# First layer's mixer woven into its input product: attention and retention by head pairs

## The chip, the cores and the metric

The kernel runs on one core of one Trainium2 chip. The metric is the device time of one execution in microseconds, lower is better; the median of several runs is compared. The kernel before took 1972.54 us (median of 3 runs, 1969.43 to 1974.33).

## What is computed

The reference is a stack of blocks on a sequence of 512 positions of width 1024, in float32: a first block (pooling, stick-breaking attention, memory attention), then two layers of mixer and convolutional GeGLU feed-forward. The change touches only the mixer of the first of these two layers, which is cut here to what matters:

```python
def retention_na_mixer(hn, w_in, ret_decay_logit, ret_gn_g, na_rpb, w_out):
    proj = hn @ w_in                                   # 512 x 1024 @ 1024 x 3584
    rq, rk, rv, rg, nq, nk, nv = jnp.split(proj, ...)  # seven parts of 512 columns, 8 heads x 64
    rq = rotary(rq); rk = rotary(rk) * 64 ** -0.5
    # decay gamma[0] for keys at or before the query, gamma[1] for keys after it
    y = bidir_scan(rq, rk, rv, rv, log_gamma[0], log_gamma[1])
    mu, var = mean and variance of y over the 64 channels of a head
    y = (y - mu) * rsqrt(var + EPS) * ret_gn_g
    ret_out = silu(rg) * y
    # 8 x 64 grid; each query sees all 8 rows and 16 columns around its own, with a bias by distance
    na_out = neighborhood_attention(nq, nk, nv, na_rpb)   # softmax
    return concatenate([ret_out, na_out]) @ w_out         # 512 x 1024 @ 1024 x 1024
```

After it, `x = x + rms_norm(m)`, and the feed-forward.

## The kernel before, in words

Activations lie with features on the 128 partitions and the 512 positions along the free dimension. A product is made by tiles of 128 output features. Each weight tile (128x1024, 512 KB) is a slot of a ring of five (RING): SyncE loads it (L264) as soon as slot q-5's product is done (slot_done), ScalarE makes its high part w_hi (hi_to, L271), VectorE the low part w_lo (lo_to, L278), and TensorE computes high x high, high x low and low x high for eight k (three, L305 to L311), 24 matmuls of 512 columns into one PSUM bank. split_ahead says how far ahead of tile t the splits are: it is an order written by hand into the programs of ScalarE and VectorE, and each engine's program is strictly in order. Normed products (in1, in2, up0, ...) start with a lead of several tiles that go k by k, while the input is still being split into a_hi and a_lo; other products start their first tile k by k.

The stage around the change, in order. "in2" has 28 tiles (four each of retention's Q, K, V, gate, and attention's Q, K, V), in banks (4 + t) % 8; VectorE evacuates each with a multiplication by the norm into p2 (L1955) and signals evac. tile_gone waits for such an evacuation. When all 28 are gone, retention runs: rotary by a swap matrix on TensorE, with cosine products on POOL and sine products on VectorE (ret_pe, ret_pool, ret_dve), V transposed (vt2), then head by head: scores of 128 keys by 512 queries in four banks, multiplied by the decay strip (weigh, L619), value matmuls (L516), evacuation (keep, L625). The strips come from the table dist by log_decay (L609, L610) and an exponential. Then the group norm over all four tiles (means by a ones matrix L526, squares, variances L529, Ln, Exp, and a refinement on VectorE, L409 to L415, L650). Then attention: V is cut into column windows and transposed (nvw, vna), and 16 units (head, half of the columns) go through scores (L692), bias, shift and maximum (L767, L771), exponential (L744), scaling by the inverse sum on VectorE (L775, L778), transposes of the weights (L702), a copy (L785), values (L715), and evacuation (L792). POOL adds bias and column mask (L756). Then the mixed tensor is split (split_mix2_act, split_mix2_dve) and "out2" starts, eight tiles one after another.

Matmuls of the mixer are in plain float32, which the trace records as two passes each. Q, K and V of a head take 64 partitions, two heads share a tile of 128.

Of the kernel before, what the change touches and what calls it, by code (L numbers as in the profile page):

```python
# [6 lines left out]
ACT = mybir.ActivationFunctionType  # L7
# [39 lines left out]
LEAD = {"in1": 2, "in2": 4, "up0": 4, "xbc": 4, "up1": 4}  # L47
# [4 lines left out]
def tile_home(name, t):  # L52
    if name == "xbc":
        return (4 + t + (1 if t >= 4 else 0) + (3 if t >= 14 else 0)) % 8
    if name == "z":
        return t % 2
    return (4 + t) % 8 if name in LEAD else t % 4

# [42 lines left out]
RET_Q, RET_K, RET_V, RET_G, NA_Q, NA_K, NA_V = 0, 4, 8, 12, 16, 20, 24  # L101
STRIP = 2 * S - P
# [26 lines left out]
def build(nc, dr, ctx, start):  # L129
# [27 lines left out]
    vt2 = at("vt2", [P, TT, RH * DH], ST + 56)  # L157
    aw2 = at("aw2", [P, 2, TT, S], ST + 64)
    strip = at("strip", [P, 2, STRIP], ST + 80)
    dist = at("dist", [P, STRIP], ST + 87)  # L160
    rope = at("rope", [P, 2, S], ST + 90.5)
    rtmp = at("rtmp", [P, 2, S], ST + 94.5)
    dec = at("dec", [P, 5, 16], ST + 98.5)
    gsq = at("gsq", [P, 4, S], 80)
    grs = at("grs", [P, 4, S], 88)
    ghalf = at("ghalf", [P, S], ST + 94.5)
    vna = at("vna", [P, 4, 2, NH * DH], ST + 64)
    bt = at("bt", [P, 2, ROWS, RPB_W], ST + 80)
    bm = at("bm", [P, 2, 4, ROWS, KEYW], ST + 84)
    cmask = at("cmask", [P, 4, KEYW], ST + 92)  # L170
    nprob = at("nprob", [P, 2, 2, ROWS * KEYW], ST + 92.5)
    npt = at("npt", [P, 2, 4, P], ST + 96.5)
    nstat = at("nstat", [P, 4, 32], ST + 100.5)
    nvw = at("nvw", [P, 4, 4, ROWS * KEYW], 64)
# [85 lines left out]
    def load_slot(sp_, q):  # L260
        name, t, part = SLOTS[q]
        if q >= RING:
            sp_.wait_ge(slot_done, q - RING + 1)
        sp_.dma_start(raw[:, q % RING, 0:slot_width(q)],  # L264
                      dr["w_" + name][t][:, part * 8 * P:part * 8 * P + slot_width(q)]).then_inc(w_load[q % RING], 16)
# [39 lines left out]
    def three(name, t, k, rhs_hi, rhs_lo, width, stop):  # L305
# [3 lines left out]
        nc.tensor.matmul(out, wh, rhs_hi[:, k, :], start=k == 0, stop=False)  # L309
# [174 lines left out]
    swap_done, cos_done, sin_done, rot_done = sem("swap_done"), sem("cos_done"), sem("sin_done"), sem("rot_done")  # L484
    strip_l, strip_e = sem("strip_l"), sem("strip_e")
    rz, ra, ry, ryc = sem("rz"), sem("ra"), sem("ry"), sem("ryc")

    g_mean, g_cent, g_sq, g_var, g_ln, g_done = sem("g_mean"), sem("g_cent"), sem("g_sq"), sem("g_var"), sem("g_ln"), sem("g_done")

    KEY_ORDER = (1, 2, 3, 0)  # L490

    def ret_pe(pe):
        for t in range(8):
            if t >= 4:
                pe.wait_ge(sin_done, t - 3)
            nc.tensor.matmul(bank[4 + t % 4][:, :], C["swap"], p2[:, t, :], start=True, stop=True).then_inc(swap_done, 1)
        for i in range(4):
            for j in range(TT):
                mm = nc.tensor.transpose(bank[i][:, j * P:(j + 1) * P], p2[:, RET_V + i, j * P:(j + 1) * P], C["ident"])
            mm.then_inc(vtp, 1)  # L500
        pe.wait_ge(vtc, 2 * TT)
        pe.wait_ge(rot_done, 8)

        def scores(h):
            b, th = DH * (h % 2), h // 2
            for j in KEY_ORDER:
                if j == 0 and h >= 2:
                    pe.wait_ge(ryc, h - 1)
                nc.tensor.matmul(zbank(h, j)[:, :], p2[b:b + DH, RET_K + th, j * P:(j + 1) * P], p2[b:b + DH, RET_Q + th, :],  # L509
                                 start=True, stop=True).then_inc(rz, 1)  # L510
# [1633 lines left out]
```

## Time and profile before

| | us |
|---|---|
| median of 3 runs | 1972.54 |
| the profiled execution, its own time | 1972.36 |
| its span | 1970.3 |
| TensorE busy | 1833.3 |
| VectorE busy | 1195.0 |
| ScalarE busy | 758.1 |
| POOL busy | 189.7 |

Times in a profile are microseconds from the span's start. PE is TensorE's matmuls, PEld its weight loads, DVE VectorE, ACT ScalarE, POOL GpSimd. L12 is line 12 of the kernel. In a row, "out<-in" are the names of what is written and read (p is p2), "x8" counts instructions, and in brackets stands how long the engine was idle before, and which instruction ended that. PEclk is the granted clock of TensorE, 1.00 being full speed.

### The profile page before, as it was taken

How to read it: one execution, taken by the hardware profiler on the slowest of the kernel's cores; microseconds unless marked ns; L12 is line 12 of the kernel's file. 1: busy time of each engine (PE TensorE's matmuls, PEld its weight loads, DVE VectorE, ACT ScalarE, POOL GpSimd, SP SyncE). 2: the span in 40 equal slices, each digit the busy share in tenths (PEclk: the TensorE clock that was granted, in tenths of full speed). 3: DMA queues.
4: the chain of work that ended last, by engine and by line, in shares of the span. 5: the costliest groups of instructions: out<-in, count | busy, mean ns of one | idle time of the engine just before them, and what ended most of it. 6: DMA issues, size and time to landing. Idle time of an engine off the chain costs nothing.

```text
span 1970.3 us, 20662 instructions
## 1 busy us (share of the span) xinstructions
PE 1833.3 (93%) x8186; PEld 1418.2 (72%) x8186; DVE 1195.0 (61%) x1647; ACT 758.1 (38%) x1278; POOL 189.7 (10%) x212
## 2 busy tenths in 40 slices
PE   7998989999878989999998999999989989999996
PEld 5885558887335768888886778677757868888885
DVE  4445554434868668866434699765676368866424
ACT  4235433212122335444323345446554245444321
POOL 0301200001123001111000000022022001111000
PEclk9999989999887989999999999999989999999998
DMA  5331002432001122333332222210001223233331
GB/s 199 97 96 54 1 11 75 137 97 85 0 13 30 64 70 93 98 96 100 98 96 83 81 75 96 65 33 24 33 32 54 96 76 96 96 97 97 95 99 62
DMA packets 42751, 147.86 MB, mean 75 GB/s; under 512 B 5152, under 2 KB 6304, under 8 KB 42528
## 3 DMA queue, kind: packets, MB, share of 16 engines
q1 hardware_dynamic: 39168, 138.43, 21.9%
q10 hardware_dynamic: 3488, 8.12, 1.2%
q8 instruction: 65, 1.06, 0.2%
q14 instruction: 30, 0.25, 0.0%
HBM read 144.44 MB, written 2.10 MB: 74 GB/s over the span
## 4 chain that ended last, share of the span: by engine, by line
PE 78%; DVE 14%; ACT 4%; issue 2%; DMA 1%; POOL 1%; ACTq 0%; DVEq 0%; POOLq 0%
PE bank L309 21%; PE bank L310 21%; PE bank L311 21%; DVE cv L1375 3%; DVE w_lo L278 2%; PE bank L509 2%; PE bank L516 1%; PE bank L1476 1%; PE bank L927 1%; PE bank L935 1%; ACT em L1576 1%; DVE bank L474 1%; PE bank L1437 1%; PE bank L920 1%; PE bank L1458 1%
## 5 line engine op out<-in xcount | busy, mean ns | idle before, releaser
L278 DVE TENSOR_TENSOR w_lo<-raw,w_hi 128x1024 fp32r<-128x1024 f32 (+1 forms) x264 | 336.6, 1277 | 532.7 <-ACT w_hi L271 532.6
L309 PE MATMUL bank<-a_hi,w_hi 128*128 128x512 f32 x1504 | 603.9, 402 | 36.1 <-DVE a_lo L374 27.8
L311 PE MATMUL bank<-a_hi,w_lo 128*128 128x512 f32 x1504 | 589.9, 392 | 0.0
L310 PE MATMUL bank<-a_lo,w_hi 128*128 128x512 f32 x1504 | 589.9, 392 | 0.0
L271 ACT ACTIVATE w_hi<-raw 128x1024 fp32r<-128x1024 f32 (+1 forms) x264 | 274.9, 1044 | 517.0 <-DMA raw<-in_w_in 172.6
L309 PEld LDWEIGHTS bank<-a_hi,w_hi 128*128 128x128 f32 x1504 | 285.7, 190 | 105.3 <-issue 22.4
L310 PEld LDWEIGHTS bank<-a_lo,w_hi 128*128 128x128 f32 x1504 | 285.6, 190 | 65.3 <-issue 6.7
L311 PEld LDWEIGHTS bank<-a_hi,w_lo 128*128 128x128 f32 x1504 | 285.0, 190 | 60.3
L309 PE MATMUL bank<-g_hi,w_hi 128*128 128x512 f32 x352 | 136.9, 389 | 0.0
L310 PE MATMUL bank<-g_lo,w_hi 128*128 128x512 f32 x352 | 136.9, 389 | 0.0
L311 PE MATMUL bank<-g_hi,w_lo 128*128 128x512 f32 x352 | 136.9, 389 | 0.0
L836 ACT ACTIVATE u<-bank,par 128x512 f32<-128x512 f32 x88 | 68.6, 780 | 176.2 <-DVE bank L474 176.2
L879 POOL TENSOR_TENSOR gv<-u 128x512 f32<-128x512 f32 x44 | 57.1, 1298 | 600.0 <-DVE u L855 600.0
L1576 ACT ACTIVATE em<-bank,lbias 128x128 f32<-128x128 f32 x256 | 70.9, 391 | 30.8 <-PE bank L1459 30.5
L1712 DVE TENSOR_TENSOR em<-em,gmat 128x512 f32<-128x512 f32 x64 | 48.7, 774 | 46.5 <-ACT em L1576 46.4
L309 PEld LDWEIGHTS bank<-g_hi,w_hi 128*128 128x128 f32 x352 | 66.1, 188 | 13.8
L311 PEld LDWEIGHTS bank<-g_hi,w_lo 128*128 128x128 f32 x352 | 66.1, 188 | 13.7
L310 PEld LDWEIGHTS bank<-g_lo,w_hi 128*128 128x128 f32 x352 | 66.1, 188 | 13.6
L1375 DVE SCALAR_TENSOR_TENSOR cv<-bank,par,cv 128x510 f32<-128x510 f32 (+1 forms) x96 | 71.7, 747 | 2.5
L855 DVE SCALAR_TENSOR_TENSOR u<-bank,par,u 128x511 f32<-128x511 f32 x88 | 66.0, 750 | 3.1
L852 DVE SCALAR_TENSOR_TENSOR u<-bank,par,u 128x511 f32<-128x511 f32 x88 | 65.1, 740 | 0.0
L474 DVE TENSOR_TENSOR bank<-bank,nrm_u 128x512 f32<-128x512 f32 x88 | 60.8, 691 | 0.9 <-PE bank L311 0.9
(347 smaller groups left out, 2197.0 us busy)
## 6 DMA issues: line engine op xcount, KB each, us to landing
raw<-in_w_up SPq DMA_DIRECT2D x88, 512.0 KB, 3.4
raw<-in_w_in SPq DMA_DIRECT2D x52, 512.0 KB, 3.5
raw<-in_w_out SPq DMA_DIRECT2D x32, 512.0 KB, 3.5
raw<-in_w_down SPq DMA_DIRECT2D x32, 512.0 KB, 3.5
raw<-in_w_xbc SPq DMA_DIRECT2D x24, 512.0 KB, 3.5
raw<-in_w_z SPq DMA_DIRECT2D x16, 512.0 KB, 3.5
raw<-in_w_down SPq DMA_DIRECT2D x16, 384.0 KB, 3.1
x<-in_xT ACTq DMA_DIRECT2D x4, 512.0 KB, 7.1
```

What stands on the lines that cost most here:

```text
L271: nc.scalar.activation(w_hi[:, q % RING, 0:w], raw[:, q % RING, 0:w], ACT.Copy).then_inc(hi_done, 1)
L278: nc.vector.tensor_tensor(w_lo[:, q % RING, 0:w], raw[:, q % RING, 0:w], w_hi[:, q % RING, 0:w].bitcast(F32), ALU.subtract).then_inc(lo_do ...
L309: nc.tensor.matmul(out, wh, rhs_hi[:, k, :], start=k == 0, stop=False)
L310: nc.tensor.matmul(out, wh, rhs_lo[:, k, :], start=False, stop=False)
L311: return nc.tensor.matmul(out, wl, rhs_hi[:, k, :], start=False, stop=stop)
L474: nc.vector.tensor_tensor(tile_bank(name, t)[:, :], tile_bank(name, t)[:, :], r, ALU.mult).then_inc(scaled, 1)
L836: nc.scalar.activation(u[:, t % 4, :], tile_bank(name, t)[:, :], ACT.Identity, scale=pcol(f"ffn_w{layer}", 3 * t + 1), bias=pcol(f"ffn_b{l ...
L852: nc.vector.scalar_tensor_tensor(out=ut[:, 1:S], in0=pt_[:, 0:S - 1], scalar=pcol(w, 3 * t), in1=ut[:, 1:S], op0=ALU.mult, op1=ALU.add).th ...
L855: nc.vector.scalar_tensor_tensor(out=ut[:, 0:S - 1], in0=pt_[:, 1:S], scalar=pcol(w, 3 * t + 2), in1=ut[:, 0:S - 1], op0=ALU.mult, op1=ALU ...
L879: nc.gpsimd.tensor_tensor(gv[:, i % 2, :], u[:, 2 * i % 4, :], u[:, 2 * i % 4 + 1, :], ALU.mult).then_inc(prod, 1)
L1375: nc.vector.scalar_tensor_tensor(out=dst, in0=tile_bank("xbc", tile)[:, a + by:b + by], scalar=pcol("conv_w", 5 * tile + tap), in1=dst, op ...
L1576: e = nc.scalar.activation(em[:, n % 4, c * P:(c + 1) * P], bank[4 + n % 2][:, c * P:(c + 1) * P], ACT.Exp, bias=lbias[:, c, d, h:h + 1])
```

## The change

The order of in2's tiles becomes IN2_ORDER: attention's Q, K, V by head pair (tiles 0 to 11), retention's K, Q, V by head pair (12 to 23), the gates (24 to 27). Tiles 8 and up use only banks 0 and 1; banks 2 to 7 belong to the mixer. Before the first step TensorE waits until tile 7 is evacuated. After it, eight attention steps go between tiles 8 to 15: the scores of the next step for two heads (each on its own 64 partitions, into its own bank), the tile, the values of the step before, the next step's windows of V and this step's transposes. Scaling by the inverse sum moves from VectorE to ScalarE, which also evacuates the windows. K and V of attention are stored by columns, so that a window is contiguous and its separate copies (nvw) go; Q is stored by blocks, which POOL's reordering did. Then eight retention steps (pair, half of the keys) go between tiles 16 to 27: four scores, four values of the step before with the output of the pair in one bank, one or two tiles, the swaps and the turned V of the next pair. Cosine and sine are applied at evacuation by VectorE (the tables are multiplied by the norm once), and the swap is taken of the sine product and added. V is multiplied by a centring matrix (identity minus 1/64 within a head) where it was transposed; so y comes out with its mean taken off, and the mean matmuls and their subtraction go. The group norm runs pair by pair, one and a half pairs behind. At the end SiLU of the gates, and "out2" starts with a lead of four tiles k by k in the order of MIX2_ORDER: attention's half first, retention's half after it; the last pair's variance lies behind the first k.

```diff
-LEAD = {"in1": 2, "in2": 4, "up0": 4, "xbc": 4, "up1": 4}
+LEAD = {"in1": 2, "in2": 4, "out2": 4, "up0": 4, "xbc": 4, "up1": 4}
...
-    if name == "z":
+    if name == "z" or name == "in2" and t >= 8:
         return t % 2
...
+IN2_ORDER = ([first + p for p in range(PAIRS) for first in (NA_Q, NA_K, NA_V)]
+             + [first + p for p in range(PAIRS) for first in (RET_K, RET_Q, RET_V)]
+             + [RET_G + p for p in range(PAIRS)])
+NA_STEPS = 2 * PAIRS
+RET_STEPS = 2 * PAIRS
+RET_TILES = [(17,), (18, 19), (20,), (21, 22), (23,), (24, 25), (26,), (27,)]
+MIX2_ORDER = (4, 5, 6, 7, 0, 1, 2, 3)
...
-        return PLAN[name]["slot0"] + max(min(t, 5) + 8, t + AHEAD) if name in LEAD else last_slot(name, t) + AHEAD
+        return PLAN[name]["slot0"] + max(min(t, 4 if name == "in2" else 5) + 8, t + AHEAD) if name in SUMS else last_slot(name, t) + AHEAD
...
+    def na_scores(pe, s):
+        p, i = s // 2, s % 2
+        tile_gone(pe, "in2", max(IN2_AT[NA_Q + p], IN2_AT[NA_K + p]))
+        if s:
+            pe.wait_ge(ns, 2 * s)
+        for r in range(2):
+            c = 2 * i + r
+            for e in range(2):
+                mm = nc.tensor.matmul(bank[4 + e][:, r * 256:(r + 1) * 256], p2[HALF[e], NA_Q + p, c * P:(c + 1) * P],
+                                      window(NA_K + p, c, parts=HALF[e]), start=True, stop=True)
...
+    def na_values(pe, s):
...
+                for e in range(2):
+                    mm = nc.tensor.matmul(bank[2][HALF[e], c * P:(c + 1) * P], vna[:, s % 2, 2 * r + f, HALF[e]],
+                                          npt[:, e, 2 * r + f, :], start=f == 0, stop=f == 1)
...
+    def ret_turn_v(pe, p):
...
+        for j in range(TT):
+            mm = nc.tensor.matmul(bank[6 if p else 3][:, j * P:(j + 1) * P], p2[:, RET_V + p, j * P:(j + 1) * P], centre[:, :],
+                                  start=True, stop=True)
...
+    def ret_scores(pe, r):
...
+            for e in range(2):
+                nc.tensor.matmul(bank[4 + 2 * jj + e][:, :], p2[HALF[e], RET_K + p, j * P:(j + 1) * P], p2[HALF[e], RET_Q + p, :],
+                                 start=True, stop=True).then_inc(rz, 1)
...
+    def two_pe(pe):
...
+            tile_pe(pe, "in2", t, a_hi, a_lo)
+        tile_gone(pe, "in2", 7)
+        na_windows(pe, 0)
+        na_scores(pe, 0)
+        for s in range(NA_STEPS):
+            if s + 1 < NA_STEPS:
+                na_scores(pe, s + 1)
+            tile_pe(pe, "in2", 8 + s, a_hi, a_lo)
+            if s:
+                na_values(pe, s - 1)
+            if s + 1 < NA_STEPS:
+                na_windows(pe, s + 1)
+            na_turn(pe, s)
+            if s == NA_STEPS - 2:
+                ret_swaps(pe, 0)
+        ret_turn_v(pe, 0)
+        tile_pe(pe, "in2", 16, a_hi, a_lo)
+        na_values(pe, NA_STEPS - 1)
+        for r in range(RET_STEPS):
+            p, half = r // 2, r % 2
+            ret_scores(pe, r)
+            if r:
+                ret_values(pe, r - 1)
+            for n, t in enumerate(RET_TILES[r]):
+                tile_pe(pe, "in2", t, a_hi, a_lo)
+                if n == 0 and half and p + 1 < PAIRS:
+                    ret_swaps(pe, p + 1)
+                    ret_turn_v(pe, p + 1)
+            if half == 0 and p:
+                ret_variance(pe, p - 1)
+        ret_values(pe, RET_STEPS - 1)
...
+    def out2_pe(pe):
+        for n, k in enumerate(MIX2_ORDER):
+            pe.wait_ge(mixlo, KT + n + 1)
+            if n == 1:
+                ret_variance(pe, PAIRS - 1)
+            for t in range(LEAD["out2"]):
...
+                mm = three("out2", t, k, a_hi, a_lo, S, n == KT - 1, MIX2_ORDER[0])
...
+        for t in range(LEAD["out2"], KT):
+            if t >= 6:
+                pe.wait_ge(g_norm, PAIRS - 2 + t - 5)
+            tile_pe(pe, "out2", t, a_hi, a_lo)
...
+        act.wait_ge(nyc, MEM_HEADS + PAIRS)
+        act.wait_ge(slot_done, last_slot("in2", 27) + 1)
+        high(0)
+        high(1)
+        square(PAIRS - 1)
+        high(2)
+        high(3)
+        nc.scalar.preload_act_table(ACT.Silu)
+        for t in range(4):
+            tile_gone(act, "in2", IN2_AT[RET_G + t])
+            nc.scalar.activation(p2[:, RET_G + t, :], p2[:, RET_G + t, :], ACT.Silu).then_inc(silu_done, 1)
+        nc.scalar.preload_act_table_set(LOGEXP)
+        roots(PAIRS - 1)
...
+        for s in range(NA_STEPS):
+            if s:
+                turned(s - 1)
+            if s + 1 < NA_STEPS:
+                for e in range(2):
+                    shift(s + 1, e)
+                invert(s + 1, 0)
+            lo_to(dve, split_ahead("in2", 8 + s))
+            if s + 1 < NA_STEPS:
+                invert(s + 1, 1)
+            take(8 + s)
+            if s and s % 2 == 0:
+                keep_na(s // 2 - 1)
+            if s == 1:
+                decay_dve(dve)
+                dve.wait_ge(dist_load, 16)
+            if s in (3, 5):
+                log_decay(s // 4)
+        turned(NA_STEPS - 1)
+        rotate(0)
+        tile(16)
+        keep_na(PAIRS - 1)
+        for r in range(RET_STEPS):
+            p, half = r // 2, r % 2
+            weigh(r)
+            if half == 0 and p:
+                keep_ret(p - 1)
+            for n, t in enumerate(RET_TILES[r]):
+                tile(t)
+                if n == 0 and half and p + 1 < PAIRS:
+                    rotate(p + 1)
+            if half == 0 and p + 1 < PAIRS:
+                log_decay(2 * p + 2)
+                log_decay(2 * p + 3)
+            if half and p:
+                norm(p - 1)
+        low(0)
+        keep_ret(PAIRS - 1)
+        for n in range(1, 4):
+            low(n)
+        norm(PAIRS - 1)
```

## Rows read from the trace of the kernel before

**Rows 1.** The page, part 1: each engine's busy time, share of the span, instructions.

```profile
PE 1833.3 (93%) x8186; PEld 1418.2 (72%) x8186; DVE 1195.0 (61%) x1647; ACT 758.1 (38%) x1278; POOL 189.7 (10%) x212
```

**Rows 2.** Busy time by stretch: length, PE, PEld, DVE, ACT, POOL, clock, DMA.

```profile
375.00:484.00 109.00, 108.84 (x481) 89.81 (x479) 39.08 (x45) 22.29 (x21) 0.00 (x0) 1.00 0.30 97
484.00:654.00 170.00, 133.43 (x465) 69.84 (x465) 132.96 (x230) 45.35 (x110) 42.52 (x48) 0.86 0.06 16
590.00:654.00 64.00, 50.59 (x245) 36.04 (x245) 53.98 (x106) 20.44 (x70) 19.57 (x28) 0.79 0.09 25
...
1300.00:1400.00 100.00, 97.01 (x526) 69.53 (x522) 64.05 (x94) 51.34 (x123) 16.91 (x11) 0.98 0.13 41
```

**Rows 3.** Waits between 484 and 654 us: waiter, releaser, total, times, longest.

```profile
PE bank L702 <- DVE nprob L778: 14.0, 11, 6.4
```

**Rows 4.** Busy time by stretch, retention's first scores.

```profile
503.00:511.20 8.20, 7.90 (x14) 3.71 (x15) 6.20 (x9) 2.15 (x3) 0.00 (x0) 0.51 0.00 1
```

**Rows 5.** Timeline of TensorE and ScalarE: start, length, instruction, idle before it.

```profile
374.88 0.39 PE L309 MATMUL bank<-a_hi,w_hi 128*128 128x512 f32 x1
...
378.69 1.06 ACT L271 ACTIVATE w_hi<-raw 128x1024 fp32r<-128x1024 f32 x1 [4.63 <-DMA raw<-in_w_in]
...
653.96 0.47 PE L309 MATMUL bank<-a_hi,w_hi 128*128 128x512 f32 x1 [1.60 <-DVE a_lo L818]
```

**Rows 6.** Timeline of VectorE, evacuations of in2's tiles (4; 5 to 9; 10; 27).

```profile
380.93 0.69 DVE L1955 TENSOR_TENSOR p<-bank,nrm 128x512 f32<-128x512 f32 x1
...
386.30 3.08 DVE L1955 TENSOR_TENSOR p<-bank,nrm 128x512 f32<-128x512 f32 x5
...
391.61 0.68 DVE L1955 TENSOR_TENSOR p<-bank,nrm 128x512 f32<-128x512 f32 x1
...
484.07 0.68 DVE L1955 TENSOR_TENSOR p<-bank,nrm 128x512 f32<-128x512 f32 x1
```

**Rows 7.** Timeline of TensorE at full clock: means, variances; one attention unit.

```profile
561.96 3.70 PE L526 MATMUL bank<-p,cst 128*128 128x512 f32 x8 [0.79 <-DVE p L625]
565.50 3.60 PE L529 MATMUL bank<-gsq,cst 128*128 128x512 f32 x8
...
631.00 0.66 PE L702 MATMUL bank<-cst,nprob 128*128 128x128 f32 x4 [0.24 <-DVE nprob L778]
631.60 1.09 PE L715 MATMUL bank<-npt,vna 128*64 128x128 f32 x8
632.62 1.13 PE L692 MATMUL bank<-p 64*128 64x256 f32 x4
```

**Rows 8.** Timeline of TensorE: first scores of two heads; SSD's paired heads among products.

```profile
507.72 1.22 PE L509 MATMUL bank<-p 64*128 64x512 f32 x2
...
1302.71 0.40 PE L311 MATMUL bank<-a_hi,w_lo 128*128 128x512 f32 x1
1303.03 1.09 PE L1476 MATMUL bank<-em,xtok 128*64 128x128 f32 x16
1304.06 1.09 PE L1424 MATMUL bank<-cst,xbc 128*128 128x128 f32 x8
...
1306.30 0.47 PE L309 MATMUL bank<-a_hi,w_hi 128*128 128x512 f32 x1
1306.62 0.39 PE L310 MATMUL bank<-a_lo,w_hi 128*128 128x512 f32 x1
```

**Rows 9.** Groups by line: count, busy us, mean ns, idle before; POOL's biases of a head.

```profile
L767 DVE SCALAR_TENSOR_TENSOR nprob<-bank,bm 128x512 f32<-128x512 f32 x16 | 11.0, 690 | 11.8 <-PE bank L702 6.2 <-POOL bm L756 5.5
...
599.63 2.86 POOL L756 TENSOR_TENSOR bm<-bt,cmask 128x256 f32<-128x256 f32 x4 [4.33 <-DVE nprob L767]
```

**Rows 10.** Timeline: group norm of one tile on VectorE; ScalarE's four SiLU.

```profile
484.21 2.19 ACT L1872 ACTIVATE p<-p 128x512 f32<-128x512 f32 x4
...
569.53 0.68 DVE L409 TENSOR_SCALAR ghalf<-bank 128x512 f32<-128x512 f32 x1
...
572.43 0.75 DVE L650 SCALAR_TENSOR_TENSOR p<-p,par,grs 128x512 f32<-128x512 f32 x1
```

More of the change, by code:

```diff
@@ new lines, in na_windows, with na_turn @@
+    def na_windows(pe, s):
+        p, i = s // 2, s % 2
+        tile_gone(pe, "in2", IN2_AT[NA_V + p])
+        if s:
+            pe.wait_ge(nvc, s)
+        for r in range(2):
+            for f in range(2):
+                mm = nc.tensor.transpose(bank[3][:, (2 * r + f) * P:(2 * r + f + 1) * P],
+                                         window(NA_V + p, 2 * i + r, f * KEYW // 2, (f + 1) * KEYW // 2), C["ident"])
+        mm.then_inc(nvp, 1)
+    def na_turn(pe, s):
+        for e in range(2):
+            un = 2 * s + e
@@ new lines, in ret_values @@
+    def ret_values(pe, r):
+        p, half = r // 2, r % 2
+        pe.wait_ge(ra, 4 * (r + 1))
+        if r == 0:
+            pe.wait_ge(nyc, MEM_HEADS + PAIRS)
+        elif half == 0 and p >= 2:
+            pe.wait_ge(g_norm, p - 1)
+        for jj in range(2):
+            j = 2 * half + jj
+            for e in range(2):
+                mm = nc.tensor.matmul(bank[2 + p % 2][HALF[e], :], vt2[p % 2][:, j, HALF[e]], aw2[:, r % 2, 2 * jj + e, :],
+                                      start=j == 0, stop=j == TT - 1)
+        mm.then_inc(rv, 1)
@@ L794, in na_dve, with turned @@
-        shift(0)
-        for un in range(NU):
-            if un + 1 < NU:
-                shift(un + 1)
-            norm(un)
-            if un:
-                turned(un - 1)
-        turned(NU - 1)
-        keep(NH - 1)
+            nc.vector.reciprocal(nstat[:, 2, 2 * un:2 * un + 2], nstat[:, 1, 2 * un:2 * un + 2]).then_inc(nrec, 1)
+        def turned(s):
+            for e in range(2):
+                dve.wait_ge(ntp, MEM_UNITS + 2 * s + e + 1)
+                nc.vector.tensor_copy(npt[:, e, :, :].rearrange("p a q -> p (a q)"), bank[6 + e][:, :]).then_inc(ntc, 1)
@@ new lines, in low @@
+        def low(n):
+            k = MIX2_ORDER[n]
+            dve.wait_ge(mixhi, KT + n + 1)
+            nc.vector.tensor_tensor(a_lo[:, k, :], mix2(k), a_hi[:, k, :].bitcast(F32), ALU.subtract).then_inc(mixlo, 1)
+        for t in range(4):
+            tile(t)
+        nc.vector.scalar_tensor_tensor(out=centre[:, :], in0=C["ones64"], scalar=-1.0 / DH, in1=C["ident"], op0=ALU.mult, op1=ALU.add)
+        for t in range(4, 8):
+            tile(t)
+        for e in range(2):
+            shift(0, e)
```

592 lines of the change are left out of this document (292 added, 300 removed).

## The prediction

> **What bounds the kernel now.** The page comes first. TensorE is busy for 93% of the span, VectorE for 61%, ScalarE for 38% [rows 1]; so time is to be had only where TensorE waits or runs slowly. The table by stage says where. From 375 to 484 us (the product "in2" from its tile 8 on) TensorE is busy for 108.8 of 109 us at a granted clock of 1.00; from 484 to 654 us (retention, then neighbourhood attention, no product beside them) it is busy for 133 of 170 us at 0.86, while the other engines are busy for 133 (VectorE), 45 and 43 us; from 654 us ("out2") it is full again [rows 2]. So the mixer's 170 us are the place: 37 us of waits, and a lower clock on a part of what is left. The waits view names the longest: 14.0 us for VectorE's softmax scaling, L778 [rows 3]; others are for the group norm and for V's evacuation. Two levels of the clock occur: after the wait for V's evacuation the stretch from 503.0 to 511.2 us runs at 0.51, which is 1.2 GHz [rows 4]; 1.00 is 2.4 GHz [rows 2].
>
> I compare two lengths, both from the first matmul of in2's tile 8 (374.88 us) to the first of out2 (653.96 us [rows 5]). Before: 653.96 - 374.88 = **279.1 us**.
>
> **The change part by part, at the full clock.**
>
> *Product.* Tiles 8 to 27 stay. VectorE's takes at 391.61 and 484.07 us are 17 tiles apart, so one is 5.44 us [rows 6]; 20 x 5.44 = **108.8**. One matmul of it is 5.44 / 24 = 0.227 us.
>
> *Neighbourhood attention.* Eight steps of two heads replace 16 units. In a unit of before, two score matmuls start 1.37 us ahead of the turn with a wait of 0.24 in it, four transposes take 0.60 (631.00 to 631.60), four value matmuls 1.02 (631.60 to 632.62) [rows 7]. A step issues four scores, four value windows to transpose, eight transposes and eight value matmuls. Transposes: 12 x 0.15 = 1.80 a step. The eight value matmuls alternate between the heads' column halves. That form stands in the trace of before, in the later SSD stage: L1476, 16 passes (each f32 matmul is recorded as two) of 128x128, two column halves in turn, runs from 1303.03 to 1304.06, 1.03 us, where the unit's 8 passes take 1.02 [rows 7, 8]. So pairs run side by side: 1.03 a step instead of 2.04. Scores: 8 passes of 256 columns, two row halves in turn, into two banks. For row halves I have only the place where head 0's last scores meet head 1's first: two passes recorded from the same 507.72 us [rows 8]. I take them as paired: four slots of 0.214 us (half of a 512-column pass, below) and 0.17 for the rest, as L1476 has over its eight slots of 0.107: 1.03. Unpaired it would be 2.0. Sum: 8 x (1.80 + 1.03 + 1.03) = **30.9**.
>
> *Retention.* A 512-column f32 matmul is two passes: 8 passes run from 561.96 to 565.50 us, 0.885 a matmul [rows 7]. Per head pair: two swaps 1.77; V turned and centred by four 128-column matmuls, priced as L715's eight passes, 1.02; 8 scores and 8 values in pairs, each group of four 4 x 0.43 + 0.17 = 1.88, so 4 x 1.88 = 7.5 (4 x 0.885 = 3.54 a group if unpaired). Four variances, one of them later: 3 x 0.885. The four mean matmuls and their centring are gone. Sum: 4 x (1.77 + 1.02 + 7.5) + 2.7 = **43.9**.
>
> *Changes of shape.* L1476 starts 0.32 us after the product matmul before it instead of 0.23, and 0.32 again leads back from transposes [rows 8]: 0.09 each. Those around the packed groups are in the 0.17; 20 returns to a product tile cost 20 x 0.09 = **1.8**. The Trainium skill (TensorEngine Tiling (Array Packing), section Key Properties) says that changing the tiling mode drains TensorE, which speaks against weaving: there are some 56 changes now. By these rows a change is about 0.1 us, 5.6 us in all, and that is what the sum holds; without a drain the time would be 5.6 us lower.
>
> *The start.* TensorE now needs tile 7 evacuated before the first window is turned (bank 3), and VectorE's program for tile 4 still splits weight slot 12 ahead of the take. That slot's buffer is free only when tile 7 is done. In the trace: ScalarE's split at 378.69 after the transfer, VectorE's behind it, the take of tile 4 at 380.93 [rows 5, 6]. The takes of tiles 5 to 7 follow at 0.60 (five in 3.08 us [rows 6]); tile 7 is gone at 383.4: **8.5 us** idle. Then scores(1) waits for both shifts of step 0: multiply-add, reduce, multiply-add are 0.72 + 0.60 + 0.69 [rows 9], **2.1 us** with the signal. After such a wait the clock is at 1.2 GHz for some 7.8 us of work [rows 4], which costs half of it: **3.9**. NA_Q, NA_K and NA_V are now stored permuted; nothing in the trace writes with an 8-element stride, so a take is 0.68 to twice that, and I keep 0.68 because the reordering copy L792 (16-element runs) took 0.68; the upper end costs 2.7 us at the start only. The bias loads move to the front: three more DMA issues at about 0.4 us on ScalarE's queue, ahead of splits with over 4 us of idle [rows 5]: nothing.
>
> *What the others must keep up with.* A step gives TensorE 5.44 + 3.86 + 0.1 = 9.4 us. VectorE in it: two shifts and reduces 2.7, two copies of turned weights 1.3, a weight split 1.2 (2.15 at most beside POOL), a take 0.7 (1.3 with the two rope products), strips and outputs 1.0: 7 to 8.5. ScalarE: four exponentials 2.0, four scalings 1.6, window 0.6, split 1.1: 5.3. POOL: the four biases 2.9 [rows 9]; up to twice that with its 8-element stride, still under 9.4. In order: turn(s-1) ends, copies 1.3, shifts 2.7, inverses and split end 6.4 us later, and the tile whose take is queued behind them ends 6.6 us later, so nothing waits; the slack is thin. In retention VectorE has 21 us per pair for TensorE's 16.3 + 10.3 + 0.9. The late points are weigh(1), (3) and (5), queued behind two strips (3.6 us); they end 2 to 3 us before the swaps that wait for them. Weight loads stay ahead: a tile's slot is freed one tile earlier, and the extra work only adds time. I take **0** for stalls inside, with 24 us (3 a step) as the upper bound.
>
> *The end.* a_hi can be overwritten only when tile 27 is done (T). VectorE then takes tile 27 and does norm(2) before low(0): 0.85, then 2.90 from the halving to the last multiply and 0.75 for that [rows 10], then 0.69, so out2 starts at T + 5.3. values(7), 1.9, lies in it: **3.4** net. The splits of before (idle 1.60 ahead of out2 [rows 5]) are covered. The lead's four k of the attention half take 4 x 12 x 0.227 = 10.9, plus the last variance 0.9: T + 17.1. The fifth k needs VectorE's keep, ScalarE's square, splits, a table load of 1.3, four SiLU of 2.2 in all [rows 10], a table load and roots (T + 13.9), VectorE's refine, gain, gate and split (T + 18.2): 1.2 of waiting. So out2 is **2.1** longer: the variance 0.9 and 1.2. The gates of pairs 0 to 2 on POOL (1.3 each) end by T + 10.5, and the silu itself no longer costs a stage.
>
> **Sum.** 108.8 + 30.9 + 43.9 + 1.8 + 8.5 + 2.1 + 3.9 + 3.4 = 203.3 us against 279.1: 75.8 less; with out2's 2.1, 73.7 less. The profiled execution took 1972.36 us (span 1970.3 and 2.1 around it), 0.2 under the median of the three runs. 1972.4 - 73.7 = 1898.7: I say **1899 us**. Where the gain comes from: 37 us of waits become 14 (8.5 + 2.1 + 3.4), the low clock costs 3.9 instead of some 16 (0.86 of 170 us withholds 24, a part of it in the waits), and pairing, with the means gone, saves some 42 us of TensorE's work.
>
> **Rivals.** (a) *Only the columns pair.* If 64-row scores run one after another, 8 x 0.97 + 8 x 1.66 = 21.0 us come back: 1920. If values don't pair either, another 8 x 1.01 + 8 x 1.66 = 21.4: 1941. For it: only one meeting of heads shows row halves together. Against: that meeting, and L1476, which does nothing else. (b) *VectorE becomes the bound in the attention steps.* Splits stretched to 2.15, slower strided writes, and the order on one queue: a step of 10.5 to 12.4 instead of 9.4 gives 1908 to 1923. For it: 0.2 us of slack in the walk. Against: operations on PSUM and the reduces are steady at 0.69 (L767 [rows 9]). (c) *Slower than before, by the clock.* The woven stretch is a mixture of f32 passes, transposes and tiles; if TensorE stayed at 1.2 GHz in it, its 185 us of work would double, 2084 us. The point of decision: 73.7 us of extra time, that is 147 us of the stretch run at the low level. For it: 590 to 654 us has 0.79. Against: there TensorE waits in each unit; 1300 to 1400 us, the same mixture with tiles, has 0.98 [rows 2]. (d) *The change hides more than I allow*: no clock loss at the start (3.9), the end waits covered (4.6), no cost of changes (5.6): down to 1885.
>
> **How the numbers follow.** Forecast, 1890 to 1908: 0.60. (b) 0.16. (a) 0.07 for rows alone, 0.03 for both. (d) below 1890: 0.06. Between 1923 and the old time by a mixture of these: 0.04. (c), or another loop of waits that eats it all: 0.04. The range for 8 in 10 takes the forecast, (b), rows of (a) and a part of (d): 1886 to 1923. About 0.3% (6 us) is what can be told from no change; every case but (c) is faster by more than that: faster 0.95, same 0.01, slower 0.04.
>
> **What the profile after would show.** Right: an idle of 8 to 9 us on TensorE after tile 7, ended by VectorE's take; then takes of product tiles 9 to 10 us apart in the attention steps; eight-pass groups of retention in about 1.9 us; a clock near 1.00 from 400 us on; out2 starting near 578 us. Wrong: groups of 3.6 us (a), TensorE waiting for VectorE's shifts or rope in most steps (b), granted clocks under 0.9 in the woven stretch (c), more than 6 us between tile 27 and out2.

## The result and the profile after

The changed kernel took **1894.97 us** (median of 4 runs, 1892.94 to 1897.02), the kernel before beside it 1972.59 us; the ratio is 0.961 (95% interval 0.960 to 0.963). The forecast was 1899, with 1886 to 1923 as its range. The profiled execution took 1892.94 us (span 1891.2).

The page of the kernel after, its part 1; TensorE is busy for 58 us less than in [rows 1]:

```profile
PE 1775.2 (94%) x8194; PEld 1387.4 (73%) x8194; DVE 1166.6 (62%) x1591; ACT 769.8 (41%) x1310; POOL 178.7 (9%) x199
```

The whole mixer now lies between 368.55 us (tile 7 done) and 571.53 (first matmul of out2). Busy time by stretch (length, PE, PEld, DVE, ACT, POOL, clock, DMA), to be read against [rows 2]:

```profile
375.00:394.00 19.00, 13.89 (x58) 10.27 (x58) 11.73 (x20) 7.37 (x23) 6.05 (x8) 0.63 0.11 30
394.00:470.00 76.00, 76.00 (x479) 59.07 (x479) 57.16 (x97) 38.95 (x96) 18.12 (x20) 1.00 0.24 76
470.00:572.00 102.00, 98.92 (x420) 62.37 (x419) 67.17 (x93) 24.56 (x30) 0.00 (x0) 1.00 0.17 57
```

Where before had 133 of 170 us busy at a clock of 0.86, TensorE is now full at 1.00 from 394 us to tile 27's end; what is left of waiting lies at the two ends. All its waits from 325 to 626 us (waiter, releaser, total, times, longest):

```profile
PE bank L594 <- DVE p L853: 9.2, 1, 9.2
PE bank L322 <- DVE a_lo L932: 3.9, 2, 3.1
PE bank L582 <- DVE nprob L867: 2.2, 1, 2.2
```

**The measure used from here on** is the length of the stage in each profile: from the first matmul of in2 to the first of up0, the next product after out2. Before it is 706.68 - 330.45 = 376.2 us, after it is 626.36 - 324.12 = 302.2, so 74.0 us less. It is steadier than a whole run: in2 starts at 324.1 to 332.7 us in the profiles of all these kernels, in which nothing ahead of in2 differs. The medians of the kernel before, timed beside them in four series, are 1972.59, 1968.34, 1970.78 and 1971.49.

### The profile page after: what moved, and what is told of

The parts are those of the page before. It is cut to its first block, busy times and chain, and to the rows that moved or that the text cites. A ratio compares the mean times of both kernels' runs of the same rounds, so it can differ in the third digit from the quotient of the medians.

```text
span 1891.2 us, 20686 instructions
## 1 busy us (share of the span) xinstructions
PE 1775.2 (94%) x8194; PEld 1387.4 (73%) x8194; DVE 1166.6 (62%) x1591; ACT 769.8 (41%) x1310; POOL 178.7 (9%) x199
## 3 DMA queue, kind: packets, MB, share of 16 engines
q8 instruction: 65, 1.06, 0.2%
## 4 chain that ended last, share of the span: by engine, by line
PE 80%; DVE 12%; ACT 5%; issue 1%; DMA 1%; ACTq 0%; POOL 0%; DVEq 0%
PE bank L322 22%; PE bank L323 22%; PE bank L324 22%; DVE cv L1552 4%; DVE w_lo L291 2%; PE bank L1653 1%; PE bank L1104 1%; PE bank L1112 1%; ACT em L1753 1%; PE bank L657 1%; DVE bank L487 1%; PE bank L1614 1%; PE bank L1097 1%; PE bank L670 1%; PE bank L1635 1%
## 5 line engine op out<-in xcount | busy, mean ns | idle before, releaser
L291 DVE TENSOR_TENSOR w_lo<-raw,w_hi 128x1024 fp32r<-128x1024 f32 (+1 forms) x264 | 337.5, 1281 | 460.6 <-ACT w_hi L284 460.3
```

The source lines that it names most:

```text
L291: nc.vector.tensor_tensor(w_lo[:, q % RING, 0:w], raw[:, q % RING, 0:w], w_hi[:, q % RING, 0:w].bitcast(F32), ALU.subtract).then_inc(lo_do ...
```

## The experiments

Each kernel is the changed one with one edit ("after, again" has none, and both_ends has two). Stage lengths and times; the number of timed runs is 4, or 2 for those marked *:

| kernel | stage, us | against after | median, us | ratio to before |
|---|---|---|---|---|
| after, again | 302.3 | | 1896.33 | 0.962 (0.960 to 0.965) |
| rows_in_blocks* | 302.3 | 0.0 | 1895.98 | 0.962 (0.958 to 0.966) |
| cols_in_blocks* | 306.4 | +4.2 | 1896.13 | 0.962 (0.959 to 0.965) |
| head_by_turns* | 330.3 | +28.0 | 1921.83 | 0.975 (0.972 to 0.978) |
| scale_on_vector | 301.6 | -0.7 | 1895.14 | 0.961 (0.960 to 0.963) |
| early_take | 298.0 | -4.3 | 1889.28 | 0.959 (0.957 to 0.961) |
| earliest_take | 292.2 | -10.1 | 1886.20 | 0.957 (0.955 to 0.958) |
| kept_busy | 300.3 | -2.0 | 1893.84 | 0.961 (0.959 to 0.964) |
| early_norm_end | 302.7 | +0.4 | 1898.46 | 0.964 (0.961 to 0.966) |
| own_square_buffer | 299.7 | -2.6 | 1890.95 | 0.959 (0.958 to 0.961) |
| out2_lead_one* | 313.1 | +10.9 | 1906.00 | 0.967 (0.964 to 0.970) |
| both_ends | 289.3 | -13.0 | 1880.30 | 0.954 (0.952 to 0.955) |

In "after, again" in2 starts at 326.36 us, and from the end of tile 7 to out2 it is 203.1 us again: the start wanders by single execution, the stage does not.

**One thing moves a stage by itself.** TensorE waits 3.08 us ahead of out2 in the kernel after. Ten of the profiles have this wait (3.07 or 3.08), after long unbroken work. In four of them (cols_in_blocks, head_by_turns, kept_busy, out2_lead_one) the granted clock fell to half, in the wait or just behind it, for 3.4 to 6.8 us, in the other six it did not. Busy time by stretch of cols_in_blocks, the columns as above (the clock, 0.50, is the third from the end):

```profile
580.60:584.02 3.42, 3.42 (x10) 2.65 (x9) 1.36 (x3) 3.39 (x6) 0.16 (x1) 0.50 0.00 0
```

From out2's first matmul to up0's it is 54.83 us in the kernel after, 55.24 in cols_in_blocks and kept_busy (0.4 more) and 56.52 in head_by_turns (1.7 more). These amounts are taken off below where they bear on the reading.

### Do the halves of the array work side by side?

The prediction's boldest term was that 64-row and 64-column products of two heads run as pairs; 42 us hung on it (21.0 for rows, 21.4 for columns). First the strict alternation is given up, then the overlap itself.

```diff
 # rows_in_blocks: scores of attention and retention, and VectorE's waits to match
-        for r in range(2):
-            for e in range(2):
+        for e in range(2):
+            for r in range(2):
```

> In the first layer, the turn between the two row halves of TensorE is given up in the scores of the attention and of the retention: all four passes of one head, then all four of the other, instead of a pass of each by turns. Nothing else changes. The length of the stage is counted from the second layer's input product's first matmul to its up product's first matmul (302.3 us now). Theory one: two halves work together only where neighbours in the queue belong to different halves. Then the eight score groups of attention go from 1.02 to about 2.0 us and the eight of retention by 1.66 us more each: 8 x 0.97 + 8 x 1.66 = 21.0 us, a stage of about 323 and a time of about 1916 us. Rival: a pass of the second half starts beside passes of the first that are still queued or running, some passes ahead; with groups of only four passes nothing is lost: 302 to 303 us, a time of about 1895.

```diff
 # cols_in_blocks: values of attention and retention
-        for r in range(2):
-            for f in range(2):
-                for e in range(2):
+        for e in range(2):
+            for r in range(2):
+                for f in range(2):
```

> The same for the two column halves: the values products of attention (sixteen passes for a pair, eight a head) and of retention (eight, four a head) are issued head after head. Theory one, neighbours only: attention's values go from 2.06 to about 3.07 us for each of eight pairs (+1.01), retention's by 1.66: 8 x 1.01 + 8 x 1.66 = 21.4 us, a stage of about 324 us and a time of about 1916. Rival, a look some four passes ahead: retention's groups lose nothing, and of attention's eight and eight passes four run alone on each side: 8 x 4 x 0.107 = 3.4 us, a stage of 305 to 306 us and a time of about 1898.

```diff
 # head_by_turns
-            ret_scores(pe, r)
-            if r:
-                ret_values(pe, r - 1)
+            for e in range(2):
+                ret_scores(pe, r, e)
+                if r:
+                    ret_values(pe, r - 1, e)
```

> Retention of a pair is taken head after head in full: scores of the first, values of the first, scores of the second, values of the second; attention stays as it is. Theory: two different halves are never side by side for long (scores use row halves, values column halves), so the sixteen half-array groups lose their overlap: 16 x 1.66 = 26.5 us and some 1.6 us for the changes of shape, a stage of about 330 us and a time of about 1923. Rival: the overlap was not what made these groups short, or other work of the stage fills the time: under 5 us, a time of 1895 to 1900.

TensorE's timeline (start, length, instruction), the scores and values of one of retention's eight steps: of the kernel after, then of rows_in_blocks, then of head_by_turns:

```profile
491.03 1.99 PE L657 MATMUL bank<-p 64*128 64x512 f32 x8
492.95 1.94 PE L670 MATMUL bank<-aw,vt 128*64 128x512 f32 x8
```

```profile
491.13 1.99 PE L657 MATMUL bank<-p 64*128 64x512 f32 x8
493.06 1.94 PE L670 MATMUL bank<-aw,vt 128*64 128x512 f32 x8
```

```profile
497.35 1.98 PE L657 MATMUL bank<-p 64*128 64x512 f32 x4
499.26 1.93 PE L670 MATMUL bank<-aw,vt 128*64 128x512 f32 x4
501.12 1.98 PE L657 MATMUL bank<-p 64*128 64x512 f32 x4
503.04 1.93 PE L670 MATMUL bank<-aw,vt 128*64 128x512 f32 x4
```

Eight passes of two heads take the 1.9 us of four passes of one head. So the pairing is real, and the rival of head_by_turns falls: its stage is 28.0 us longer. That this is just the 28 of the theory is luck. Two of the sixteen groups still pair, because nothing stands between their two heads, retention's first scores and its last values. Here they are in head_by_turns:

```profile
468.46 1.99 PE L657 MATMUL bank<-p 64*128 64x512 f32 x8
...
595.39 1.94 PE L670 MATMUL bank<-aw,vt 128*64 128x512 f32 x8
```

So there are 14 groups more, of 1.88 us each from start to start on average ((501.12 - 497.35) / 2): 26.3 us, which is what out2's start is later by (600.41 - 380.49 against 571.53 - 377.93, from the first window on). The other 1.7 us are the clock behind out2's wait, told above.

But the strict theory of the order falls as well: with all four passes of one half ahead of the four of the other, the group is no longer than before (1.93 us against 1.92, and the stage 302.3). In rows_in_blocks two passes are recorded from one start, as in [rows 8]; its timeline up to 491.20 us ends with

```profile
491.13 0.71 PE L657 MATMUL bank<-p 64*128 64x512 f32 x2
```

The records don't name the head, but eight passes in the time of four leave only this reading: passes of the second half start beside those of the first that stand before them in the queue. How far this reaches, cols_in_blocks tells, with eight passes of one half ahead of eight of the other (first the attention values of the kernel after, then of cols_in_blocks):

```profile
400.69 1.09 PE L620 MATMUL bank<-npt,vna 128*64 128x128 f32 x16
401.72 0.66 PE L594 MATMUL bank<-cst,p 128*128 128x128 f32 x4
```

```profile
404.74 1.58 PE L620 MATMUL bank<-npt,vna 128*64 128x128 f32 x16
406.25 0.65 PE L594 MATMUL bank<-cst,p 128*128 128x128 f32 x4
```

From start to start 1.51 us instead of 1.03: 0.48 more. A single pass starts 0.109 us behind the one before it on its half (a slot). With a reach of four passes the group would be four slots longer (0.44), with a reach of one seven (0.76). The single passes show four: up to 405.20 us only four have started,

```profile
404.74 0.65 PE L620 MATMUL bank<-npt,vna 128*64 128x128 f32 x4
```

from 405.23 to 405.61 us they start two by two, four on either half, and from 405.72 us the last four start one by one. Eight such groups give 3.9 us; 0.4 more is the clock behind out2's wait, which is why the stage (306.4) lies just above the 305 to 306 that were expected. Retention's groups of four and four lose nothing. The time of its two runs doesn't show the difference (1896.13); the stage does.

### Is VectorE close to being the bound?

```diff
 # scale_on_vector: ScalarE's norms(s) dropped; on VectorE, for each head
+            for r in range(2):
+                c = 2 * un + r
+                m = nc.vector.tensor_scalar(nprob[:, un % 4, r, :], nprob[:, un % 4, r, :], nstat[:, 2, c:c + 1], None, ALU.mult)
+            m.then_inc(nnorm, 1)
```

> Attention's scaling by the softmax's row sum goes back to VectorE (the reciprocal and two scalings for each pair), and ScalarE no longer does it. VectorE's part of an attention step is 7 to 8.5 us of 9.2 and grows by 1.2 to 1.6 us (up to 3 where it takes turns with GpSimd). Theory: TensorE with its queued products keeps the step, 0 to +5 us over the eight pairs: a stage of 302 to 307 us, a time of 1895 to 1900. Rival: VectorE becomes the bound of each step, 9.2 to 11.5 us: +8 to +18 us, a time of 1903 to 1913.

Busy time from 403 to 440 us, four attention steps, of the kernel after and of scale_on_vector:

```profile
403.00:440.00 37.00, 37.00 (x243) 29.06 (x241) 31.51 (x57) 22.01 (x60) 15.28 (x16) 1.00 0.28 87
```

```profile
403.00:440.00 37.00, 37.00 (x242) 29.14 (x241) 34.63 (x70) 14.84 (x40) 10.88 (x15) 1.00 0.28 85
```

VectorE goes from 31.5 to 34.6 of 37 us and TensorE stays at 37.0: no wait appears. The rival is out, and with it the prediction's (b): the 0.8 us that VectorE got for each step ((34.63 - 31.51) / 4) are not felt. From the end of tile 8 to up0 every group starts 1.07 or 1.08 us sooner behind the first window than in the kernel after, so not one step differs. The -0.7 us lies ahead of that: the first wait is 9.60 us instead of 9.22, but the granted clock is back at 1.00 from 386.1 to 389.5 us, so that the second scores take 1.14 us and not 2.08:

```profile
387.88 1.14 PE L582 MATMUL bank<-p 64*128 64x256 f32 x8 [2.19 <-DVE nprob L866]
```

No edit stands for this.

### What makes the wait at the start?

A take is VectorE's evacuation of a tile, a split the making of a weight slot's low part. VectorE's timeline of the kernel after (in brackets: idle before, releaser):

```profile
369.20 0.68 DVE L851 TENSOR_TENSOR p<-bank,nrm 128x512 f32<-128x512 f32 x1
369.80 0.28 DVE L936 SCALAR_TENSOR_TENSOR centre<-cst 128x128 f32<-128x128 f32 x1
373.25 1.23 DVE L291 TENSOR_TENSOR w_lo<-raw,w_hi 128x1024 fp32r<-128x1024 f32 x1 [3.16 <-ACT w_hi L284]
374.39 1.99 DVE L853 TENSOR_TENSOR p<-bank,nrm 128x512 f32<-128x512 f32 x2
376.21 0.68 DVE L851 TENSOR_TENSOR p<-bank,nrm 128x512 f32<-128x512 f32 x1
376.81 1.06 DVE L853 TENSOR_TENSOR p<-bank,nrm 128x512 f32<-128x512 f32 x1
```

The takes of tiles 4 to 7 stand behind a split (L291), that of slot 12, whose buffer is free only when tile 7 is done (368.55), and whose weights then have to be loaded and split by ScalarE. Two edits of the one number that says how far the splits run ahead:

```diff
 # early_take (3) and earliest_take (0)
-        return PLAN[name]["slot0"] + max(min(t, 4 if name == "in2" else 5) + 8, t + AHEAD) if name in SUMS else ...
+        return PLAN[name]["slot0"] + max(min(t, 3 if name == "in2" else 5) + 8, t + AHEAD) if name in SUMS else ...
```

> One number: split_ahead of in2 uses min(t, 3) where the changed kernel has min(t, 4), so VectorE's take of tile 4 no longer stands behind the split of slot 12. Theory: the 9.2 us in which TensorE waited for tile 7's take shrink to about 1.3 (signal and one strided take of 1.1), and with so short a wait the clock stays at 2.4 GHz, which gives back another 3 to 4: 10 to 12 us less than the changed kernel, 1883 to 1885. Rival: the split of slot 12, now inside the first attention step on VectorE and ScalarE, delays shift(1) or the scaling and the wait moves there: under 5 us of gain. Second rival: the wait for the two shifts (2.2 us) alone is enough to lower the clock: 8 us of gain.

> The turning of K and V ahead of the takes is cut down so that VectorE's first takes (tiles 3 to 7) don't stand behind the split that waits for tile 6. Base: a gap of 9.22 us after tile 7 on TensorE, 4.70 with the cut of one slot less, which saved 4.3 us of the stage. Theory: the gap falls to the end of one take, about 1.3 us, and the fall of the clock behind it goes with it: a stage of 291 to 293 us, a time of 1884 to 1886. Rival: the splits that are now late hold back scores(0) and (1) instead, and the gain stays at 3 to 5 us: a stage of 297 to 299, a time of about 1889.

(What earliest_take moves is the weight splits, by the same number: those of slots 9 to 12 come four tiles later than in the kernel after.)

TensorE's timeline behind tile 7, of early_take:

```profile
377.65 1.12 PE L594 MATMUL bank<-cst,p 128*128 128x128 f32 x4 [4.70 <-DVE p L853]
```

and of earliest_take:

```profile
373.42 0.66 PE L594 MATMUL bank<-cst,p 128*128 128x128 f32 x4 [1.67 <-DVE p L853]
374.01 1.13 PE L582 MATMUL bank<-p 64*128 64x256 f32 x8
377.33 1.13 PE L582 MATMUL bank<-p 64*128 64x256 f32 x8 [2.19 <-DVE nprob L867]
378.40 0.80 PE L322 MATMUL bank<-a_hi,w_hi 128*128 128x512 f32 x1
378.99 0.63 PE L323 MATMUL bank<-a_lo,w_hi 128*128 128x512 f32 x1
```

early_take missed: the gap became 4.70 us, not the 1.3 I had written down. I had not followed the next split of the queue: tile 3's take stands behind slot 11's, which waits for tile 6 in the same way, one tile sooner. With both out of the way (earliest_take) the gap is 1.67 and the stage 10.1 us shorter: 7.6 of it from the gap, the rest from the clock, which is now low only from 378.4 us, for some 3.5 us. The rival (the late splits hold back something else) finds no wait in the trace. Which of the four splits are needed for it beyond 11 and 12 was not tried.

**The clock behind the wait** was tested by itself: nine matmuls whose result nobody reads, put into the gap.

```diff
 # kept_busy
+        tile_gone(pe, "in2", 0)
+        for _ in range(9):
+            nc.tensor.matmul(bank[4][:, :], C["ones"], p2[:, NA_Q, :], start=True, stop=True)
         tile_gone(pe, "in2", 7)
```

> Nine f32 matmuls of 512 columns that nobody reads are put into TensorE's wait for tile 7's take (they write bank 4, which is free). The wait itself stays: 9 x 0.885 is 8.0 of its 9.2 us. Theory: what follows runs at 2.4 GHz, so windows, scores and the first third of tile 8 take half as long: 3 to 4.5 us less than the changed kernel, 1891 to 1892. Rival: the clock falls in the wait for the shifts anyway: no difference. A result above the changed kernel would say that the added matmuls delay the scores.

TensorE of the kernel after, and of kept_busy:

```profile
377.93 1.11 PE L594 MATMUL bank<-cst,p 128*128 128x128 f32 x4 [9.22 <-DVE p L853]
378.97 2.08 PE L582 MATMUL bank<-p 64*128 64x256 f32 x8
383.24 2.08 PE L582 MATMUL bank<-p 64*128 64x256 f32 x8 [2.19 <-DVE nprob L867]
385.25 0.79 PE L322 MATMUL bank<-a_hi,w_hi 128*128 128x512 f32 x1
```

```profile
377.09 7.88 PE L689 MATMUL bank<-p,cst 128*128 128x512 f32 x18
386.62 0.66 PE L594 MATMUL bank<-cst,p 128*128 128x128 f32 x4 [1.65 <-DVE p L856]
387.21 1.14 PE L582 MATMUL bank<-p 64*128 64x256 f32 x8
390.53 2.08 PE L582 MATMUL bank<-p 64*128 64x256 f32 x8 [2.19 <-DVE nprob L870]
392.54 0.79 PE L322 MATMUL bank<-a_hi,w_hi 128*128 128x512 f32 x1
```

The windows and the first scores run at 2.4 GHz (0.66 and 1.14 us instead of 1.11 and 2.08), but in the next wait, 2.19 us, the clock falls: behind it the scores take 2.08 again. It is back sooner, so tile 8 gains 1.1 us; with the 1.4 of windows and scores that is 2.5. The first window starts 0.15 us later and 0.4 is lost to the clock behind out2's wait, so 2.0 us came back, not 3 to 4.5. The cost of the low clock is shown, its cure by filler work is worth half; removing the wait (earliest_take) is worth five times as much.

### What makes the wait at the end?

```diff
 # early_norm_end: norm(2) moved from ahead of low(0) to behind low(1); low(4) ahead of the last pair's gate
-        for n in range(1, 4):
-            low(n)
+        low(1)
+        norm(PAIRS - 2)
+        low(2)
+        low(3)
```

> Order of VectorE's program at the end only: low(0), keep, low(1) come ahead of norm(2), and low(4) ahead of the last pair's gate product. Theory: out2 starts about 1.9 us after tile 27 (behind values(7)) instead of 5.2, and the fifth k of out2 waits no longer than before: 3 to 4 us less, 1891 to 1892. Rival: the end is set by the chain through SiLU, its two table loads and the last norm on ScalarE, so that what out2 gains at its start it loses at its fifth k: 0 to 1 us.

out2 did start right behind values(7), but then the waits stood elsewhere. TensorE's timeline of early_norm_end (out2's first matmul, the last variance, the fifth k):

```profile
576.78 0.50 PE L322 MATMUL bank<-a_hi,w_hi 128*128 128x512 f32 x1
...
582.62 1.10 PE L676 MATMUL bank<-gsq,cst 128*128 128x512 f32 x2 [2.78 <-ACT gsq L774]
...
593.38 0.50 PE L322 MATMUL bank<-a_hi,w_hi 128*128 128x512 f32 x1 [1.47 <-DVE a_lo L932]
```

The last variance (L676) reads gsq, which ScalarE may write only when norm(2) has left it; its square (L774) waited 5.62 us for the norm that I had moved (L926). So nothing was gained (+0.4), near the rival's 0 to 1 us; but the rival's chain of table loads and SiLU was late because the square ahead of it was. So I gave the last pair's square a buffer of its own (rtmp, free by then):

```diff
 # own_square_buffer, besides: low(1), low(2), norm(PAIRS - 2), low(3); low(4) as in early_norm_end
+    def sq_of(p):
+        return rtmp[:, 0, :] if p == PAIRS - 1 else gsq[:, :]
...
-            nc.scalar.activation(gsq[:, :], p2[:, RET_V + p, :], ACT.Square).then_inc(g_sq, 1)
+            nc.scalar.activation(sq_of(p), p2[:, RET_V + p, :], ACT.Square).then_inc(g_sq, 1)
...
         def roots(p):
             act.wait_ge(g_var, p + 1)
+            if p == PAIRS - 1:
+                act.wait_ge(g_norm, p)
```

> The end of the mixer with the third pair's norm behind two of the low halves, and the last pair's square written to a buffer of its own, so that ScalarE no longer waits for norm(2) there. Theory: of the 3.08 us gap ahead of out2 and the 0.84 us ahead of the fifth k most goes: a stage of 298 to 299.5 us, a time of about 1891 to 1892. Rival: the last pair's norm chain (square, root, refine, SiLU, turn) is as long as the time saved, and the wait only moves to the fifth k: 301.5 to 302.5, a time of 1895.

The same two places of out2 in own_square_buffer's timeline:

```profile
570.62 0.50 PE L322 MATMUL bank<-a_hi,w_hi 128*128 128x512 f32 x1
...
584.00 0.50 PE L322 MATMUL bank<-a_hi,w_hi 128*128 128x512 f32 x1 [1.26 <-DVE a_lo L937]
```

One wait of 1.26 us is left of 3.08 and 0.84: 2.66 less, and the stage is 2.6 shorter. The stage, 299.7, is just above what I had put down (298 to 299.5): a part moved to the fifth k, where ScalarE's root now waits 0.95 us for norm(2) on VectorE. This norm also became slower: two of its instructions take 1.67 us each, where the kernel after has 0.69 and 0.75, and they run while POOL makes the gates of the pairs before. VectorE's and POOL's timelines of own_square_buffer:

```profile
575.43 1.67 DVE L428 SCALAR_TENSOR_TENSOR grs<-gsq,grs 128x512 f32<-128x512 f32 x1
577.13 1.67 DVE L931 SCALAR_TENSOR_TENSOR p<-p,par,grs 128x512 f32<-128x512 f32 x1
```

```profile
575.23 3.02 POOL L572 TENSOR_TENSOR p<-p 128x512 f32<-128x512 f32 x2 [136.34 <-ACT p L835]
```

The 1.9 us are more than the root's wait. That the gates are the cause was not tried by itself; both_ends has the same two rows of 1.67 us beside its gates.

```diff
 # out2_lead_one
-LEAD = {"in1": 2, "in2": 4, "out2": 4, "up0": 4, "xbc": 4, "up1": 4}
+LEAD = {"in1": 2, "in2": 4, "out2": 1, "up0": 4, "xbc": 4, "up1": 4}
```

> The product out2 of the first layer runs its four leading tiles for each k as now, but only one tile leads instead of four, so that a k step ahead of the last pairs takes about 0.68 us on TensorE instead of 2.72. Theory: the wait for the fifth k, 0.84 us now, grows by what the four steps are shorter (4 x 2.04 = 8.2 us less work ahead of it), since the variance and the norms of the last pairs end at the same time: a stage longer by 7 to 8 us, about 310 us, a time of about 1903. Rival: the last pairs' norms are not what ends last there, and the stage stays within 1.5 us of 302.3.

The fifth k started 12.9 us after out2's first matmul, exactly as in the kernel after (571.53 to 584.45): the last pair's norms set it, and the four leading tiles are what fills the time. In those 12.9 us 36 matmuls less are done (8.2 us), and behind the wait of 6.78 us the clock is at 0.50 for 6 us, which I had left out: 15 matmuls in 6.07 us instead of 3.4. Together 10.9 us instead of 7 to 8. Its timeline at out2's start and at the fifth k:

```profile
574.35 0.50 PE L322 MATMUL bank<-a_hi,w_hi 128*128 128x512 f32 x1 [3.08 <-DVE a_lo L932]
...
587.25 0.79 PE L322 MATMUL bank<-a_hi,w_hi 128*128 128x512 f32 x1 [6.78 <-DVE a_lo L932]
```

### Both ends together

> The last two together: the earliest takes and the square's own buffer. Theory: gains at two ends of the stage that don't touch each other add up: a stage of 287 to 290 us, a time of 1880 to 1883. Rival: one of them gives nothing by itself; then the stage is that of the better of the two alone.

earliest_take and own_square_buffer in one kernel: 13.0 us less, where the two alone give 10.1 and 2.6. The gains add up: the two ends don't touch each other. At 1880.30 us it is the fastest of all, 0.954 of the kernel before, and its interval (0.952 to 0.955) lies below that of the changed kernel.

## Why the prediction was right, step by step

- **The sum.** From tile 8's turn to out2: 203.3 us predicted, 571.53 - 368.55 = 203.0 measured. out2: 2.1 longer predicted; measured (626.36 - 571.53) - (706.68 - 653.96) = 2.1. The stage: 73.7 less predicted, 74.0 measured. That 203.3 comes so near is in part luck: the start is 0.9 above its terms, TensorE's work 0.9 and the end 0.3 below theirs. The prediction's 1899 against 1894.97: the profile of before started in2 6.3 us later than that of after, for which no edit stands. By whole runs the gain was 1972.59 - 1894.97 = 77.6 us here and 1968.34 - 1896.33 = 72.0 in the series with the kernel run again; the 73.7 lies between.
- **Where the gain is.** From tile 8's turn to out2 it is 279.1 - 203.0 = 76.1 us. Waits went from 36.6 us (170.00 - 133.43, [rows 2]) to 14.5 (9.22 + 2.19 + 3.08), 22 of the 76. The rest is work that takes less time: pairs, a higher clock, the mean matmuls gone. Only retention's pairs were measured by themselves (26.3 us for 14 of 16 groups); no run takes the weaving itself back.
- **Work of TensorE** (product, attention, retention, changes): 185.4 predicted. 203.0 less the three waits (9.22, 2.19, 3.08) and 4.0 of low clock leaves 184.5. An attention step is 9.21 us (values at 400.69, 409.91, 419.12) where I had 9.4; retention's groups are 1.92 and 1.87 from start to start where I had 1.88.
- **The rows pair, too** (the one term for which the trace of before had only two passes to show): right, by head_by_turns. My picture of it, halves that must alternate, was too narrow: rows_in_blocks.
- **Changes of shape.** The 14 groups that head_by_turns has more cost 1.88 us each; four passes of 512 columns are 4 x 0.4425 = 1.77 (3.54 for eight in [rows 7]), which leaves 0.11 a group for the change, near the 0.09 of [rows 8].
- **The start**: 9.22 for 8.5, 2.19 for 2.1, 4.0 for 3.9. The cause named (slot 12's split ahead of tile 4's take) was half of it: without it 4.70 us are left (early_take), and slot 11's split, which the prediction did not name, holds tile 3's take in the same way (earliest_take). The 0.7 too little is the strided write: I kept 0.68 a take, and the three L853 in the row took 3.05 together (1.99 and 1.06).
- **The clock's 3.9** I had priced after a wait of 7.3 us in [rows 4]. Behind 9.22 and 2.19 us it came out alike: windows 0.46, scores 0.95 and 0.94, tile 8 1.65.
- **The end**: 3.08 for 3.4, 0.84 for 1.2; the fifth k at T + 18.0 for T + 18.2 (T = 566.43, tile 27's end). The reason given, the norm in front of low(0), was half of it: the buffer gsq ties the last variance to the same norm, which I had not seen and early_norm_end brought out.
- **Nothing waits inside**: right. TensorE is busy for 76.00 of 76 us of the attention steps. I had 7 to 8.5 us of VectorE a step; it is 31.5 / 37 x 9.21 = 7.8. The slack that I had called thin is 1.4 us a step.
- **Rivals.** (a) falls by the rows of L657 and L670, (b) by scale_on_vector, (c) by a clock of 1.00 from 394 us. (d) did not happen by itself: the clock cost 4.0 and the end's waits 3.9. Further edits could cover a part (own_square_buffer 2.6 of the end).

The Trainium skill (TensorE: Matmul & The Clock Gate, section The mechanism) says that only weight loads are pulled ahead and that matmuls start and end strictly in program order. By that rule rows_in_blocks would have lost at least three slots in each group, 8 x 3 x 0.214 + 8 x 3 x 0.43 = 15.5 us; its stage is 302.3 us as before, so this trace speaks against the rule for passes on different halves.

## What to carry to other kernels

When 64-wide products of two heads stand in one queue, put both heads of a pair within a few passes of each other; strict turns aren't needed, but in retention one head's values between the two heads' scores lost it all. When a stage is woven into another, its inside fills by itself; what is left lies at its two ends, and there every instruction queued ahead of the releaser counts: here weight splits in front of takes, whose buffers were not free yet, cost 10 us with the clock behind the wait. Before you move a step earlier on its engine, look for a buffer that it shares with the one you want to let pass. And before you call a microsecond the effect of an edit, look at the granted clock behind each wait of the profile.

## What was unexpected of the hardware

- Passes on the second half of the array start beside queued ones of the first: no loss with four ahead, 0.48 us with eight ahead, where the first four start alone and the last four too.
- VectorE's evacuation of 128x512 with an 8-element stride in its output (L853) takes 1.05 to 1.16 us, the one in runs of 16 elements (L851) 0.68, the unbroken one (L855) 0.69. The Trainium skill (SBUF — State Buffer, section Door 1: The DMA port swizzle) gives lines of 16 bytes and a penalty for each new one; a stride of 32 bytes is beyond that, and the trace agrees in direction.
- The clock fell at two short waits close together. In kept_busy TensorE had worked without a wait, waited 1.65 us, worked 1.7 and waited 2.19: the windows and scores between the waits ran at full clock (0.66 and 1.14), the next scores took 2.08. In earliest_take (1.67, then 2.19) and both_ends (1.42, then 2.19) the scores behind the second wait still took 1.13 us, and the product behind them 0.63 a matmul. Whether the wait of 2.19 us would have done it alone was not tried.
- The same wait of 3.08 us, after long work, was followed by a low clock in four of ten profiles and not in the other six.
